# Merged kernel, two transformer blocks on one core: tokens laid out chunk by chunk, and the first attention's fills made of wide products

## The reference

```python
(x_rnn, g_rnn, dq, dk, dv, fq, fk, fv, f_logit, gates) = jnp.split(h @ w_in, IN_SPLITS, axis=-1)
o_diff = diff_attention(dq, dk, dv, lam, rel_bias)
y_diff = rmsnorm(o_diff, diff_subln_g) * (1.0 - lam_init)      # a norm per head
o_fox  = forgetting_attention(fq, fk, fv, log_f)
g = jax.nn.sigmoid(gates + gate_b)                              # 3 x 1024 columns
m = g[0] * (y_rnn @ w_br_rnn) + g[1] * (y_diff @ w_br_diff) + g[2] * (y_fox @ w_br_fox)
x = x + m @ w_out
```

## Time and profile before

| | |
|---|---|
| median of 3 runs | 1811.76 us (1809.37 to 1812.85) |
| profiled execution, its own time | 1815.71 us |
| its span, first to last instruction | 1813.7 us |
| TensorE matmul busy | 1542.5 us (85%) |
| VectorE busy | 802.7 us (44%) |
| ScalarE busy | 585.5 us (32%) |
| mean granted TensorE clock | 0.931 of full |

### The profile page before, as it was taken

The page is one execution under the profiler, slowest core; times in us unless marked ns, Lnnn a source line. Parts: engine busy times, 40 slices in busy tenths (PEclk is TensorE's granted clock), DMA queues, the critical chain, the costliest instruction groups (busy, mean ns, idle before and its releaser), DMA issues.

```text
span 1813.7 us, 32970 instructions
## 1 busy us (share of the span) xinstructions
PE 1542.5 (85%) x14712; PEld 1153.6 (64%) x14712; DVE 802.7 (44%) x1646; ACT 585.5 (32%) x1043; POOL 76.7 (4%) x87
## 2 busy tenths in 40 slices
PE   8999999999999999975666666999999966666575
PEld 7989998999798888532323333798796533333232
DVE  6896668887485875210101100557764201011011
ACT  5765546665444654000000000545642000000001
POOL 1020001000030101000000000001010000000000
PEclk9999999999999999989888888999999978888878
DMA  6543456555473568999999999953589999999997
GB/s 263 184 145 140 152 186 226 192 186 190 162 297 120 206 255 355 415 430 430 429 431 429 430 430 429 371 192 136 205 342 412 429 430 429 431 429 431 429 431 301
DMA packets 45837, 567.38 MB, mean 313 GB/s; under 512 B 6672, under 2 KB 7216, under 8 KB 10496
## 3 DMA queue, kind: packets, MB, share of 16 engines
q1 hardware_dynamic: 40176, 552.62, 74.3%
q0 software_dynamic: 3744, 12.03, 1.9%
q10 hardware_dynamic: 1776, 0.62, 0.1%
HBM read 564.18 MB, written 1.05 MB: 312 GB/s over the span
## 4 chain that ended last, share of the span: by engine, by line
PE 62%; DMA 30%; DVE 3%; another core or an unknown queue 3%; ACT 1%; issue 0%; SPq 0%; DVEq 0%; ACTq 0%
DMA slab<-in_slabs 29%; PE bank L608 10%; PE bank L610 10%; PE bank L609 10%; PE bank L652 8%; PE bank L1163 6%; PE bank L653 4%; PE bank L1215 3%; PE bank L1233 1%; PE bank L975 1%; PE bank L1034 1%; DMA sm<-in_fb 1%; PE bank L1140 1%; PE bank L998 1%; DVE wl L1255 1%
## 5 line engine op out<-in xcount | busy, mean ns | idle before, releaser
L1163 PE MATMUL bank<-slab,xe 128*32 128x256 f32 x4096 | 314.2, 463 | 155.5 <-DMA slab<-in_slabs 155.5
L1255 DVE TENSOR_TENSOR wl<-slab,wh 128x1024 fp32r<-128x1024 f32 (+1 forms) x286 | 347.4, 1228 | 130.4 <-ACT wh L1945 130.4
L1945 ACT ACTIVATE wh<-slab 128x1024 fp32r<-128x1024 f32 (+1 forms) x286 | 296.1, 1046 | 190.6 <-PE bank L610 148.0
L1163 PEld LDWEIGHTS bank<-slab,xe 128*32 128x32 f32 x4096 | 143.6, 127 | 305.3 <-DMA slab<-in_slabs 198.2
L608 PE MATMUL bank<-htb,wh 128*128 128x256 f32 x768 | 219.9, 286 | 2.8 <-DVE wl L1255 2.7
L609 PE MATMUL bank<-htb,wh 128*128 128x256 f32 x768 | 217.3, 283 | 0.0
L610 PE MATMUL bank<-htb,wl 128*128 128x256 f32 x768 | 217.2, 283 | 0.0
L652 PE MATMUL bank<-htb,wh 128*128 128x512 f32 x576 | 209.8, 405 | 0.0
L1215 PE MATMUL bank<-slab,ha 128*32 128x256 f32 x2048 | 141.7, 425 | 70.9 <-DMA slab<-in_slabs 69.8
L2335 ACT ACTIVATE ta<-bank 128x256 f32<-128x256 f32 x32 | 12.3, 384 | 501.3 <-PE bank L1163 501.3
L653 PE MATMUL bank<-htb,wl 128*128 128x256 f32 x576 | 161.6, 281 | 0.0
(11 more groups left out here) (392 smaller groups left out, 2353.3 us busy)
## 6 DMA issues: line engine op xcount, KB each, us to landing
slab<-in_slabs SPq DMA_DIRECT2D x251, 2048.0 KB, 47.9
slab<-in_slabs SPq DMA_DIRECT2D x23, 1024.0 KB, 9.7
bias<-in_bias POOLq DMA_DIRECT2D x32, 192.0 KB, 3.1
bias<-in_bias POOLq DMA_DIRECT2D x8, 256.0 KB, 5.8
x<-in_x SPq DMA_DIRECT2D x2, 512.0 KB, 4.4
rg<-in_rg POOLq DMA_DIRECT2D x1, 1024.0 KB, 10.5
bt<-in_rel POOLq DMA_DIRECT2D x1, 768.0 KB, 14.4
fg<-in_final_g POOLq DMA_DIRECT2D x1, 512.0 KB, 3.8
```

The source lines that it names most:

```text
L1163: t = e.matmul(bk[bank][32 * j:32 * j + 32, 0:256], XE[:, c, :], w[:, k, 256 * j:256 * j + 256], start=(c == 0), stop=(c == 7))
L1255: e.tensor_tensor(lo, src, hi.bitcast(F32), ALU.subtract).then_inc(*dve_l.mark(p))
L1945: e.activation(hi, src, ACT.Copy).then_inc(*act_h.mark(p))
```

## The change

- `Two` lays the chunks of `HT` out one behind the other, high part and low part of a chunk side by side (1 KB each, 512 columns in one run). `HT` keeps its 16 pages. All other tiles keep theirs.
- The weights of `fq`, `fk` and the gates are taken as `BLOCKS` in place of `PAIRS`; the 32 fills are `block`s of 128 output channels, each in a bank of its own: 7, 5, 7, 3, and from the fifth on 7 and 3 in turn.
- VectorE reads each fill's bank with `sides`, ahead of that step's `split`, into `QF`, `KF` or `GT`, and marks ("fa", "f", k). The banks and the forgetting scores wait on that mark. ScalarE's copies are gone, and its 24 tanh work in place in `GT`, one per fill, behind the mark.
- In `head_norm` the square stays behind unit 4's values, the sum and scaling move behind unit 5's, nothing stands behind unit 6's, and reciprocal and product move behind unit 7's. ScalarE's square root moves behind unit 6's output.

```diff
@@ piece_list
-    add("fq", 0, PAIRS)
-    add("fk", 0, PAIRS)
+    add("fq", 0, BLOCKS)
+    add("fk", 0, BLOCKS)
     for i in range(6):
-        add("gates", i, PAIRS)
+        add("gates", i, BLOCKS)
@@ class Two
-            if lo - hi == n and cols == 256:
-                self.both = row(name + "b", hi, 2 * n * cols, F32R).rearrange("p (s n c) -> p s n c", s=2, n=n)
+            if lo == hi:
+                self.both = row(name, hi, 2 * n * cols, F32R).rearrange("p (n s c) -> p s n c", s=2, n=n)
                 self.h, self.l = self.both[:, 0, :, :], self.both[:, 1, :, :]
-    HT = Two("ht", 8, 16, 8)
+    HT = Two("ht", 8, 8, 8)
-    bank_f, bank_l = fill_banks(sched_f, 0, 2), fill_banks(sched_l, 0, 0)
+    bank_f, bank_l = {k: (7, 5, 7, 3)[k] if k < 4 else 3 if k % 2 else 7 for k in range(32)}, fill_banks(sched_l, 0, 0)
@@ tensor_program, fox_scores
-            for j in range(4):
-                P.wait_ge(*s_l["rows", j])
-            P.wait_ge(*act_s["fk", 1])
+            P.wait_ge(*s_l["rows", 3])
+            P.wait_ge(*dve_s["fa", "f", 7])
@@ tensor_program, first_fill
-            piece(p, b, k % 2, 2, 4, HT)
-            if k % 2:
-                reader[b] = [(act_s, ("fk", k // 2 - 2) if 4 <= k < 8 else ("fill", "f", k))]
+            block(p, b, HT)
+            reader[b] = [(dve_s, ("fa", "f", k))]
@@ vector_program, head_norm
             e.tensor_tensor(SQ, O8, O8, ALU.mult).then_inc(*dve_s.mark("osq"))
-            V.wait_ge(*dve_s.now)
+            yield
+            V.wait_ge(*dve_s["osq"])
             e.reduce_sum(c_ss, SQ, axis=AX).then_inc(*dve_s.mark("osum"))
@@ vector_program, the loop over sched_f
             if kind == "f":
+                V.wait_ge(*pe_w[fills_f[i][0]])
+                dst = QF[:, i, :] if i < 4 else KF[:, i - 4, :] if i < 8 else GT[:, i - 8, :]
+                sides(dst, bank_f[i], ("fa", "f", i))
                 split(fills_f[i][0])
@@ scalar_program, first_fill
             split(fills_f[k][0])
-            if k % 2 == 0:
-                return
-            A.wait_ge(*pe_w[fills_f[k][0]])
-            b = bank_f[k]
-            if k < 8:
-                dst, n = (QF, k - 1) if k < 4 else (KF, k - 5)
-                t = e.activation(dst[:, n:n + 2, :], two(bk[b][:, :]), ACT.Copy)
-            else:
+            n = k - 8
+            if n >= 0:
                 A.wait_ge(*dve_s["hb"])
-                for n in (k - 9, k - 8):
-                    t = e.activation(GT[:, n, :], bk[b][:, (n % 2) * 256:(n % 2 + 1) * 256], ACT.Tanh,
-                                     bias=c_hb[:, 16 + n:17 + n], scale=0.5)
-            t.then_inc(*act_s.mark(("fk", k // 2 - 2) if 4 <= k < 8 else ("fill", "f", k)))
+                A.wait_ge(*dve_s["fa", "f", k])
+                e.activation(GT[:, n, :], GT[:, n, :], ACT.Tanh, bias=c_hb[:, 16 + n:17 + n],
+                             scale=0.5).then_inc(*act_s.mark(("fill", "f", k)))
@@ scalar_program, the loop over sched_f
-                if i == 5:
+                if i == 6:
                     A.wait_ge(*dve_s["oms"])
                     e.activation(c_ss, c_ss, ACT.Sqrt).then_inc(*act_s.mark("ort"))
```

## The result

The changed kernel took 1821.33 us (median of 4 runs, 1821.06 to 1822.61), the kernel before 1811.21 us on the same chip (1809.37 to 1812.85): a ratio of 1.0052, 95% interval 1.0041 to 1.0064 (this ratio and those below are as recorded; the quotient of these two medians is 1.0056). It is 10.1 us slower by the medians, where I had forecast 2.6 with a range that ended at 1820.5. The sign was right, the time was not. Three executions of a later comparison, one of them of "maximum first" and two of the kernel before, lasted over 2100 us and are left out of the ratios, though not of the medians, which they move by less than 0.3 us.

The account below looks back on a forecast made before the run. TensorE was taken to bound the first attention and the layers up to the experts. Won 4.0 + 3.2 + 0.3 = 7.5 us, lost 4.4 + 1.0 + 3.0 + 1.7 = 10.1: net +2.6, 1814.4 us; range 1807 to 1820.5.

Parts of the forecast that it names:

- The sign: Whole kernel: slower by net 2.6 us; chances 0.46 slower, 0.34 the same, 0.20 faster.
- layout: Blocks of two layers: one run of columns makes a wide-narrow couple 7 ns shorter, 576 couples, 4.0 us won.
- clock: Behind the pause at fill 2: TensorE runs a stretch at half clock, 1.7 us lost, bounds 0 and 3.4.
- units 2 and 3: First attention: TensorE waits shortly for low parts behind VectorE's sums, 1.0 us lost, bounds 0 and 2.5.
- wide products in the fills: First attention's fills: 8 couples of 347 ns replace 24 products of 120 ns, 3.2 us won, bounds 1.6 and 4.0.
- head norm's sum: Unit 6's turn: the sum no longer stands with the square ahead of the copy, 0.3 us won.
- pause at fill 2: First attention's start: fill 2 waits for fill 0's sum, behind VectorE's bias products, 4.4 us lost, bounds 3.5 and 5.0.
- pause at the end: Before the turned heads: the head norm's 1.8 us now come behind unit 7's values, 3.0 us lost, bounds 2.4 and 3.5.
- Rival 2: TensorE products: columns alone set their price, so layout brings nothing and fills 1.6 us; 1820.0 us, chance 0.12.
- The wait in front of fill 10: Unit 2: piece 10 is ready at 7.4 us behind fill 7's end, TensorE wants it at 6.8; about 0.6 us wait.
- Rival 1: Fill 2: VectorE's backlog ends sooner, so the first pause is small and the kernel faster; 1808.3 us, chance 0.20.
- Rival 3: First attention: VectorE becomes the bound, some 0.6 us in each of ten units; about 1820.5 us, chance 0.10.

Follow-up runs that it names:

- maximum first: Changed kernel with fill 2 in bank 6, head norm's product behind unit 6's values, and the maximum ahead of the low part before a unit's scores: 1811.65 us, ratio 0.9990.
- layout undone: Changed kernel with high and low part of a chunk 8 KB apart again, so wide products read two runs: 1822.01 us, ratio 1.0052 to the kernel before.
- head norm alone: Kernel before with only the head norm's edit (square, sum and product a unit later each, square root behind unit 6's output): 1816.60 us, ratio 1.0016.
- wide first: Changed kernel with each block's eight wide products issued first, then its eight narrow ones: 1818.58 us, ratio 1.0035 to the kernel before.
- low part first: Changed kernel with fill 2 in bank 6, head norm's product behind unit 6's values, and each low part ahead of the fill's sum: 1828.35 us, ratio 1.0080.
- bank 6: Changed kernel with fill 2 in bank 6 in place of bank 7, which no sum has to free: 1815.87 us, ratio 1.0020 to the kernel before.

## Why the prediction was wrong

The pauses and their causes stood. The layout's gain, the fills' gain and the clock did not: of the 7.6 us between +2.6 and +10.2, the layout is 4.0, the fills 1.6 and the clock 2.5, less 0.5 that units 2 and 3 came out better.

| term | predicted | measured | from |
|---|---|---|---|
| layout | -4.0 | 0.0 | ten blocks 28.27 both; layout undone |
| wide products in the fills | -3.2 | -1.6 | fills 2 to 4 at full clock 8.50 for 8.79, -0.13 and -1.57 of the table above, less the head norm's 0.37 |
| head norm's sum | -0.3 | -0.4 | head norm alone |
| pause at fill 2 | +4.4 | +4.6 | 5.58 - 0.97 |
| units 2 and 3 | +1.0 | +0.5 | 10.47 - 9.97, fills' gain inside |
| pause at the end | +3.0 | +2.9 | 3.69 - 0.80 |
| clock | +1.7 | +4.2 | 2.65 and 1.54 in this execution |
| sum | +2.6 | +10.2 | |

**The layout, the failed step.** "In one run a couple should take 227 + 120 = 347 ns." The 227 ns came from products in one run of columns, but these products also stood in a row of equals and streamed weights in place of tokens. I laid the whole difference to the first, and called a loss excluded and a gain likely; the layout undone shows that it has no share (28.28 us for ten blocks against 28.27), and wide first shows that the order has 4 of the 6 ns. Rows that differ in several things price none of them. This step alone carries 4.0 us, and the same 347 ns sat in the fills, where 353 gives the lower bound of 1.6 us that I had worked out, and which was measured. The rule of the Trainium skill that I had weighed ("TensorE: Matmul & The Clock Gate", "Back-to-back issue gap"), that the distance depends on the columns alone, would have been the right choice on the layout; the runs agree with it there (399 ns either way), and differ in that the order of the products moves a couple from 353 to 349 ns, which it does not have. Rival 2, that the layout brings nothing and the fills 1.6, gave 1820.0 us at a chance of 0.12; it was right on both, and what it lacks to 1821.3 is the clock.

**The clock.** I took one half-clock stretch of 1.7 us and held the second pause for a bound, 3.4 in all. Both pauses did it: 1.54 us at the end, and at the first 2.65 in the profiled execution, where fills 2 to 4 ran for a whole 4.22 us and part of the next 6.90 at half, and 1.5 to 1.6 in two of the experiments. So the price of one stretch was near where it was short; the second stretch was missing from the sum, and the first was longer in the profiled execution than the one in the earlier trace rows. The pause of 4.49 us in the earlier trace rows, from the experts, gave the mechanism and not the size; here pauses of 4.6, 2.9, (head norm alone) 2.4 and (low part first) 2.2 and 2.1 us were all followed by half clock, and with idle products in them the first two were not.

**What was right.** Fill 2's wait for fill 0's sum, on VectorE without a gap behind the bias products: 4.6 us for 4.4, and bank 6 removes it. The 1.8 us of the head norm moved behind the last sum: 2.9 for 3.0, and one yield less removes it. The wait in front of fill 10:

```profile
153.44 0.50 PE L652 MATMUL bank<-ht,wh 128*128 128x512 f32 x1 [0.40 <-DVE wl L1253]
```

0.40 us for the 0.6 foreseen, and the maximum ahead of the low part removes it. It is the only wait of TensorE for another engine's result that the trace of after lists from 130 to 232 us, apart from loads of weights. Rival 1 did not come: VectorE's backlog was there again. Rival 3 did not either, though with the sums doubled about half of the added work was no longer hidden. That time behind the first attention is carried on in full was right as well: 10.2 us at the feed-forward, 10.2 at layer 0's experts. But that layer 0's blocks began 6.4 us later in the profile (511.22 for 504.79), where 5 to 7 were foreseen, is luck: it is 10.2 us of loss less the 3.8 us of the start.

Open is how the 4 ns of the order come about, where the other 2 of the 6 ns are (a wide product in a row takes 231 ns of distance in a block, 227 in the rows I had used), and why the first half-clock stretch was longer in some executions.

## What to carry to other kernels

When a reader moves from one engine to another, ask at each place of the list, and first of all at its beginning and end, what the new reader has to finish before it; thirty sums cost about half a microsecond between other work, while one at the beginning and 1.8 us of head norm moved to the end cost 7.5 us of pauses and 4.2 of clock. Price a form of instruction from a row that differs from it in one thing alone, or measure it in a kernel that changes only that. Before an engine gets more work, follow what the queues wait for in turn: the same sums ahead of the low parts cost little, behind them 17 us.

## What the runs showed of the hardware

- A 512-column float32r product took 399 ns whether its moving columns lay in one run or in two 8 KB apart.
- Alternating products of 512 and 256 columns took 353 ns a couple, eight of one and then eight of the other 349 (231 and 119 ns of distance).
- Pauses of 2.4, 2.9 and 4.6 us of TensorE, in stages that were busy without a break, were each followed by products at 1.2 GHz: a mean granted clock of 0.61, 0.57 and 0.50 over the next 3.6 to 4.2 us, which cost 1.5, 1.5 and, in different executions, 1.5 to 2.65 us. A wait of 2.06 us was followed by half clock too ("low part first", 0.81 on the mean from 157 to 166 us). With idle products in the pause (4.69 us at a granted clock of 1.00) it did not fall.
- One small transfer at the start took 15.27 us in one profiled execution and 11.66 in another (9.9 to 16.7 over all of them), and moved all that followed by 3.8 us. Two spans are to be compared from a product behind it.
